# A two-layer trunk on one core: duos of the state-space layer spaced evenly, and the turn of its outputs written in the order of the tokens

## The chip, the cores and the metric

The kernel runs on one core of a Trainium2 chip. The metric is the device time of one execution in microseconds (us). Lower is better.

## The reference, cut to what matters

Two decoder layers work on 256 tokens of width 2048 in float32, each a token mixer, a SwiGLU feed-forward part and a gated per-layer embedding. The mixer of the second layer is the part that the change touches:

```python
def _s5_mixer(h, w_in, a_re, a_im, log_dt, b_re, b_im, c_re, c_im, d, w_out):
    u = (h @ w_in).astype(f32)                        # 256 x 2048
    ...
    bu = b_bar * u, per group of 16 channels, 64 complex states
    _, s = lax.associative_scan(_lin_combine, (a, bu), axis=1)
    y = Re(C s) + d * u                               # 256 x 2048
    g = jax.nn.gelu(y)
    val, gate = jnp.split(g @ w_out, 2, axis=-1)      # w_out is 2048 x 4096
    return val * jax.nn.sigmoid(gate)
```

## The kernel before, in words

All large products are done as a list of 783 weight tiles of 256 x 512 float32 (512 KB), `ORDER`, that every engine walks through. A float32 product is made of three: SyncE loads tile t into one of four slots (`RAW`), ScalarE rounds it to the high part (`WHI`, L779), VectorE subtracts that to get the low part (`WLO`, L1057), and TensorE multiplies the high part by both parts of the activations (8 matmuls, L1566) and the low part by the high part of the activations (4 matmuls, L1572). `section()` is this step on ScalarE and VectorE, and `until(t)` does it for all tiles to t + 2. A load of tile t waits for the low part of tile t - 4. ScalarE's rounding of tile t waits until TensorE is done with tile t - 4.

The stage `win` (h @ w_in) is tiles W0 to W0 + 31, eight for each of four columns of 512, and `out1` (g @ w_out) begins at W0 + 32. Below, "tile 40" is the tile W0 + 40. The work of the state-space layer is fitted between these tiles. Its 128 groups are taken in eight duos (d = 0 to 7) of 16 groups. TensorE does `into_states(d)` (64 small matmuls, L1758, the increments of the states) after tile `INTO_AT[d]`, and `out_of_states(d)` (96 small matmuls, L1775 and L1783, the outputs) after tile `OUT_AT[d]`. The order of the loops over g and the lists of places are written by hand. For each duo the chain is:

1. `into_states(d)` on TensorE;
2. `scan(d)` on VectorE, ten instructions, which begins with the transpose of the increments out of PSUM (`CV`, L1459) when VectorE has come to g = INTO + 1, that is after the low part of tile INTO + 3;
3. `out_of_states(d)` on TensorE, four tiles after the increments; for d = 6 and 7 it writes banks that are free only when VectorE has transposed the increments of duo 7;
4. `take_y(d)` on ScalarE at OUT + 1 (GELU, `YP`, L974);
5. `turn_y(d)` on VectorE at OUT + 2 (32 x 32 transposes, `YG`, L1485), after the low part of tile OUT + 4;
6. `y_high(d)` on ScalarE at OUT + 2 (L981), the high part of the operand, ahead of the rounding of tile OUT + 5;
7. `y_low(d)` on VectorE at OUT + 3 (L1490), after the low part of tile OUT + 5.

`out1` needs y as its operand: a tile (0, j), the j-th tile of column 0, waits for `y_low(j)`:

```python
if n == 0 and stage == "out1":
    pe.wait_ge(y_ready, j + 1)
```

`EARLY` orders the first three columns of `out1` so that tiles with a small j come first. Column 2 uses bank 6, and its first tile waits for `take_y(5)`.

The columns of u go to the states through DRAM: `turn_u(n)` on VectorE at 8n + 9 (L1451), `store_u(n)` (`ud`, L958) and `spread_u(n)` (`UP`, L966, four issues that wait for the store to land) on ScalarE's queue at 8n + 11 and 8n + 13. GpSimd's queue loads the tables TQ, TD, TK and TE of each duo at `TQ_AT`, `TD_AT`, `TK_AT` and `TE_AT`: 3.25 MB for a duo, beside 2 MB of weights in four tiles.

The layout of `YG` is (b, i, k): two blocks, the 8 tokens of a chunk, the 32 chunks. A token is 8k + i. So `y_high` and `y_low` read elements 128 bytes apart and write without gaps.

Of the kernel before, what the change touches and what calls it, by code (L numbers as in the profile page):

```python
# [6 lines left out]
F32 = mybir.dt.float32  # L7
F32R = mybir.dt.float32r
I32 = mybir.dt.int32
ACT = mybir.ActivationFunctionType  # L10
ALU = mybir.AluOpType
AX = mybir.AxisListType

P = 128
TOK = 256
# [16 lines left out]
T = 8  # L32
NC = TOK // T
# [11 lines left out]
PROJ_AT = 4  # L45

EARLY = [(n, j) for j in range(4) for n in (0, 1)] + [(2, j) for j in range(4)]
EARLY += [(n, j) for j in range(4, 8) for n in (0, 1, 2)]

def plan():
    order = []
    for name, cols, depth in STAGES:
        if name == "out1":
            order += [(name, n, j) for n, j in EARLY]
            order += [(name, n, j) for n in range(3, cols) for j in range(depth)]
# [11 lines left out]
def start(stage, n=0):  # L69
    return INDEX[stage, n, 0]  # L70
# [98 lines left out]

W0 = start("win")  # L170
U_AT = [W0 + 8 * n + 9 for n in range(NT)]
INTO_AT = [W0 + g for g in (16, 19, 24, 27, 32, 34, 40, 42)]
OUT_AT = [W0 + g for g in (20, 23, 28, 31, 36, 38, 44, 46)]

OUT_BANK = [6] * (DUOS - 2) + [4, 4]
Y_AT = [t + 2 for t in OUT_AT]
DSET = [0, 1, 2, 0, 1, 0, 1, 0]

G0 = start("gate0")
TQ_AT = [(G0 + 1, G0 + 3), (G0 + 13, G0 + 15)]  # L180
TD_AT = [(G0 + 5, G0 + 7), (G0 + 18, G0 + 20), (W0, W0 + 2)]
TK_AT = [(G0 + 9, G0 + 11), (G0 + 22, G0 + 24), (W0 + 4, W0 + 6)]
TE_AT = [G0 + 12, G0 + 26]
TQ_AT += [(W0 + g, W0 + g + 1) for g in (17, 20, 25, 28, 33, 35)]
TD_AT += [(W0 + g, W0 + g + 1) for g in (22, 26, 30, 37, 39)]
TK_AT += [(W0 + g, W0 + g + 1) for g in (24, 30, 32, 39, 41)]
TE_AT += [W0 + g for g in (20, 23, 28, 31, 36, 38)]

def set_before(d):  # L190
# [14 lines left out]
def trunk(nc, x, p, norm_mix, norm_ffn, norm_ple, norm_final, gm_w_in, gm_ln_g, gm_ln_b, gm_w_s, gm_b_s,  # L205
# [3 lines left out]
    with ctx:  # L209
        def sem(name):  # L210
            return ctx.enter_context(nc.semaphore(name))

        KBYTE = 1024
# [5 lines left out]
        def place(name, shape, dt=F32, at=None):  # L219
            size = 4  # L220
            for s in shape[1:]:
                size *= s
            if at is None:
                at = top[0]
                top[0] += (size + 31) // 32 * 32
                assert top[0] <= base + ARENA, name
            return nc.alloc_sbuf_tensor_at(name, shape, dt, offset=at)
# [3 lines left out]
        OP = place("OP", [P, 40, 2 * TOK], F32R)  # L231
# [3 lines left out]
        s_at = top[0]  # L235
# [28 lines left out]
        def f_view(name, shape, off, dt=F32):  # L264
            size = 4
            for s in shape[1:]:
                size *= s
            assert off * KBYTE + size <= 48 * KBYTE + 512, name
            return place(name, shape, dt, at=f_at + int(off * KBYTE))
# [65 lines left out]
        UP = [op_view(f"UP{i}", [P, 2, QB, QP, NC], 24 + 4 * i) for i in range(2)]  # L335

        YP = place("YP", [P, 2, T, 2, CH], at=s_at)
        YG = place("YG", [P, 2, T, NC], at=s_at + 2 * KBYTE)
        VAL = f_view("VAL", [P, 2, NW], 0)

# [89 lines left out]
        yg_ready = sem("yg_ready")  # L431
        y_hi = sem("y_hi")
        y_ready = sem("y_ready")
# [333 lines left out]
        def _(act):  # L767
            A_ = nc.scalar
# [200 lines left out]
            def take_y(d):  # L969
                act.wait_ge(out_of, d + 1)  # L970
                if d:
                    act.wait_ge(yg_ready, d)
                for g in range(2):
                    last = A_.activation(YP[:, :, :, g, :].rearrange("p b i c -> p b c i"),  # L974
                                         PS[:, OUT_BANK[d] + g, 0:2 * P].rearrange("p (b c i) -> p b c i", b=2, i=T),
                                         ACT.Gelu_apprx_tanh)
                last.then_inc(yp_ready, 1)

            def y_high(d):
                act.wait_ge(yg_ready, d + 1)  # L980
                A_.activation(OP[:, 2 * d:2 * d + 2, 0:TOK].rearrange("p b (k i) -> p b k i", i=T),  # L981
                              YG[:, :, :, :].rearrange("p b i k -> p b k i"), ACT.Copy).then_inc(y_hi, 1)

            for g in range(5, 62):
                until(W0 + g)
# [9 lines left out]
                for d in range(DUOS):  # L995
                    if W0 + g == Y_AT[d]:
                        y_high(d)
                    if W0 + g == OUT_AT[d] + 1:
                        take_y(d)
# [46 lines left out]
        def _(dve):  # L1046
            step = Chain(dve, dve_chain)
            V_ = nc.vector
# [274 lines left out]
            for n in range(NT):  # L1323
# [10 lines left out]
                for th in range(2):  # L1334
                    for m in range(QB):
                        h = QB * n + m
                        c = slice(P * m, P * m + P)
# [143 lines left out]
            def turn_y(d):  # L1481
                dve.wait_ge(yp_ready, d + 1)
                if d:
                    dve.wait_ge(y_ready, d)
                V_.transpose(YG[:, :, :, :].rearrange("p b i k -> p (b i k)"),  # L1485
                             YP[:, :, :, :, :].rearrange("p b i g c -> p (b i g c)")).then_inc(yg_ready, 1)

            def y_low(d):
                dve.wait_ge(y_hi, d + 1)
                V_.tensor_tensor(OP[:, 2 * d:2 * d + 2, TOK:2 * TOK].rearrange("p b (k i) -> p b k i", i=T),  # L1490
                                 YG[:, :, :, :].rearrange("p b i k -> p b k i"),
                                 OP[:, 2 * d:2 * d + 2, 0:TOK].bitcast(F32).rearrange("p b (k i) -> p b k i", i=T),
                                 ALU.subtract).then_inc(y_ready, 1)

            dve.wait_ge(core_ready, 1)
            until(W0 + 8)
# [2 lines left out]
            for g in range(7, 62):  # L1499
                until(W0 + g)  # L1500
                for n in range(NT):
                    if W0 + g == U_AT[n]:
                        turn_u(n)
                for d in range(DUOS):
                    if W0 + g == INTO_AT[d] + 1:
                        scan(d)
                    if W0 + g == Y_AT[d] + 1:
                        y_low(d)
                    if W0 + g == OUT_AT[d] + 2:
                        turn_y(d)  # L1510
                if W0 + g == end("out1", 1):
                    gated("out1", 1, VAL[:, :, :])
# [41 lines left out]
        def _(pe):  # L1554
# [191 lines left out]
            def into_states(d):  # L1746
                n, i = d // 2, d % 2
                pe.wait_ge(tq_in[i], 32 * (n + 1))
                pe.wait_ge(up_in, 64 * (n + 1))
                if d >= 2:  # L1750
                    pe.wait_ge(inc_free, d - 1)
                for bl in range(2):
                    for q in range(QP):
                        at = ST * (QP * bl + q)
                        for g in range(2):
                            for half in range(2):
                                state = ST * g + 32 * half
                                last = T_.matmul(PS[state:state + 32, 4 + i, at:at + ST], UP[n % 2][:, g, 2 * i + bl, q, :],  # L1758
                                                 TQ[i][:, bl, q, :, state:state + 32], start=True, stop=True)
                last.then_inc(in_done, 1)  # L1760

            def out_of_states(d):
                n, i, tab = d // 2, d % 2, DSET[d]
                pe.wait_ge(td_in[tab], 64 * (DSET[:d].count(tab) + 1))
                pe.wait_ge(sd_ready, d + 1)
                if d:
                    pe.wait_ge(yp_ready, d)
                if OUT_BANK[d] == 4:
                    pe.wait_ge(inc_free, DUOS)
                bank = OUT_BANK[d]  # L1770
                for bl in range(2):
                    f = slice(P * bl, P * bl + P)
                    for g in range(2):
                        for q in range(QP):
                            T_.matmul(PS[NC * q:NC * q + NC, bank + g, f], UP[n % 2][:, g, 2 * i + bl, q, :],  # L1775
                                      TKK[tab][:, bl, 2 * q + g, :], start=(bl == 0), stop=False, skip_group_check=True)
                for bl in range(2):
                    f = slice(P * bl, P * bl + P)
                    for ri in range(2):
                        for q in range(QP):  # L1780
                            for g in range(2):
                                half = slice(ST * g, ST * g + ST)
                                last = T_.matmul(PS[NC * q:NC * q + NC, bank + g, f], SD[i][half, ri, QP * bl + q, :],  # L1783
                                                 TD[tab][half, bl, q, ri, :], start=False, stop=(ri == 1), skip_group_check=True)
                last.then_inc(out_of, 1)

            for t in range(W0, INDEX["out1", 2, 7] + 1):
# [12 lines left out]
                for d in range(DUOS):  # L1800
                    if t == INTO_AT[d]:
                        into_states(d)
                    if t == OUT_AT[d]:
                        out_of_states(d)
# [55 lines left out]
```

## Time and profile before

| what | value |
|---|---|
| time, median of 3 runs | 2246.61 us (2244.24 to 2249.15) |
| the profiled execution: its own time | 2250.04 us |
| its span | 2248.0 us |
| TensorE busy with matmuls | 2229.2 us (99%) |
| VectorE busy | 1442.2 us (64%) |
| ScalarE busy | 1021.1 us (45%) |
| DMA over the span | 235 GB/s |
| granted TensorE clock, mean | 0.998 |

Tile 16 starts in this trace at 1166.45 us and tile 48 at 1289.36 us. A time is read against the start of the span. The difference of own time and span, 2.04 us, lies around the profiled program.

### The profile page before, as it was taken

To read this page: it belongs to the slowest core of one execution; us is meant where nothing else is said; L and a number is where in the kernel's file an instruction comes from. 1 tells how busy PE (TensorE), PEld (TensorE's weight loads), DVE (VectorE), ACT (ScalarE), POOL (GpSimd) and SP (SyncE) were. 2 spreads that over 40 slices of the span, in tenths; PEclk is the share of its full clock that TensorE was granted. 3 is DMA by queue.
4 is the path that set the end of the run, shared out by engine and by line. 5 is a ranking of instruction groups with operands and counts; after the bars stand their busy time and mean duration, and the time that the engine had idled before them with its cause. 6 is when DMAs were issued, how large, how long until landed. Compare 5 with 4: busy or idle time off the path is not lost.

```text
span 2248.0 us, 28342 instructions
## 1 busy us (share of the span) xinstructions
PE 2229.2 (99%) x11250; PEld 1834.4 (82%) x11250; DVE 1442.2 (64%) x1590; ACT 1021.1 (45%) x1233; POOL 494.0 (22%) x469
## 2 busy tenths in 40 slices
PE   9999999999999999999999999999999999999998
PEld 7888878888888888888887788888888888888886
DVE  7878776667666666666668766555555445555665
ACT  5544454444434444445444455444444344444444
POOL 1245236455665544301003100000000000000001
PEclk9999999999999999999999999999999999999999
DMA  8667799888887888887779877677766667777764
GB/s 288 188 206 232 242 274 269 245 245 254 248 247 219 259 259 245 249 256 265 236 250 338 302 220 222 198 222 217 217 213 214 191 195 221 219 215 232 227 213 143
DMA packets 348517, 527.90 MB, mean 235 GB/s; under 512 B 105968, under 2 KB 125312, under 8 KB 347744
## 3 DMA queue, kind: packets, MB, share of 16 engines
q1 hardware_dynamic: 337296, 488.50, 71.4%
q0 software_dynamic: 8320, 30.75, 3.8%
q10 hardware_dynamic: 2768, 6.83, 0.9%
q8 instruction: 89, 1.46, 0.3%
q14 instruction: 44, 0.36, 0.1%
HBM read 474.10 MB, written 51.90 MB: 234 GB/s over the span
## 4 chain that ended last, share of the span: by engine, by line
PE 90%; DVE 4%; DMA 3%; issue 1%; ACT 1%; SPq 1%; DVEq 0%; ACTq 0%
PE PS L1566 58%; PE PS L1572 29%; DVE WLO L1057 1%; DMA HT<-zd 1%; DMA RAW<-in_s_w_out 1%; DMA RAW<-in_ffn_w 1%; ACT WHI L779 0%; PE PS L1597 0%; DMA RAW<-in_s_w_in 0%; PE PS L1669 0%; PE PS L1837 0%; PE PS L1838 0%; PE PS L1836 0%; DVE CB L1469 0%; PE PS L1660 0%
## 5 line engine op out<-in xcount | busy, mean ns | idle before, releaser
L1566 PE MATMUL PS<-WHI,OP 128*128 128x512 f32 x6208 | 1541.3, 390 | 1.4 <-ACT WHI L779 1.1
L1057 DVE TENSOR_TENSOR WLO<-RAW,WHI 128x1024 fp32r<-128x1024 f32 x783 | 1022.2, 1317 | 660.8 <-ACT WHI L779 657.9
L1566 PEld LDWEIGHTS PS<-WHI,OP 128*128 128x128 f32 x6208 | 1161.7, 188 | 248.1 <-issue 6.6
L779 ACT ACTIVATE WHI<-RAW 128x1024 fp32r<-128x1024 f32 x783 | 825.4, 1061 | 936.0 <-PE PS L1572 759.6
L1572 PE MATMUL PS<-WLO,OP 128*128 128x512 f32 x3104 | 830.7, 389 | 3.8 <-DVE WLO L1057 3.6
L1572 PEld LDWEIGHTS PS<-WLO,OP 128*128 128x128 f32 x3104 | 582.2, 188 | 127.1 <-DVE WLO L1057 6.1
L763 POOL TENSOR_TENSOR ON<-X,GF 128x1024 f32<-128x1024 f32 x3 | 9.9, 3291 | 947.8 <-DVE X L1406 947.8
L666 POOL TENSOR_TENSOR TA<-BRAW,FAC 128x64 f32<-128x64 f32 x16 | 8.2, 512 | 259.8 <-DMA BRAW<-in_s_b_im 259.8
L1069 DVE TENSOR_TENSOR OP<-HT,OP 128x512 fp32r<-128x512 f32 x50 | 34.9, 739 | 46.7 <-ACT OP L794 46.7
L794 ACT ACTIVATE OP<-HT 128x512 fp32r<-128x512 f32 x50 | 28.8, 624 | 65.3 <-DMA HT<-zd 65.3
L827 ACT ACTIVATE S<-PS,RC 128x512 f32<-128x512 f32 x66 | 41.8, 685 | 36.5 <-PE PS L1572 36.5
L1083 DVE SCALAR_TENSOR_TENSOR OP<-HT,VEC,OP 128x128 fp32r<-128x128 f32 x96 | 26.3, 347 | 32.1 <-ACT OP L803 32.1
L803 ACT ACTIVATE OP<-HT,VEC 128x256 fp32r<-128x256 f32 x48 | 20.5, 498 | 35.9 <-DMA HT<-zd 35.9
L1393 DVE SCALAR_TENSOR_TENSOR Z<-PS,RC,S 128x512 f32<-128x512 f32 x44 | 30.9, 744 | 6.0 <-PE PS L1572 5.2
L1124 DVE BATCH_NORM_STATS2 STAT<-X 128x6 f32<-128x512 f32 x54 | 34.1, 673 | 0.0
L1108 DVE STREAM_TRANSPOSE ZT<-Z 128x512 f32<-128x512 f32 x50 | 32.6, 691 | 0.9
L913 ACT ACTIVATE EXPF<-PS 128x128 f32<-128x128 f32 (+7 forms) x128 | 17.8, 264 | 33.2 <-PE PS L1669 33.2
L698 POOL TENSOR_TENSOR TA<-CT,LAMA 128x512 f32<-128x512 f32 x16 | 18.1, 1134 | 60.8 <-DMA CT<-cd 60.8
L701 POOL TENSOR_TENSOR TA<-CT,LAMA 128x512 f32<-128x512 f32 x16 | 31.0, 1936 | 1.3
L700 POOL TENSOR_TENSOR DT<-TA,TB 128x512 f32<-128x512 f32 x16 | 31.0, 1936 | 1.3
L685 POOL TENSOR_TENSOR QT<-TA,TB 128x512 f32<-128x512 f32 x16 | 30.5, 1908 | 1.3
L702 POOL TENSOR_TENSOR TB<-CT,LAMA 128x512 f32<-128x512 f32 x16 | 29.9, 1869 | 0.0
(213 smaller groups left out, 961.6 us busy)
## 6 DMA issues: line engine op xcount, KB each, us to landing
RAW<-in_ffn_w SPq DMA_DIRECT2D x528, 512.0 KB, 4.7
RAW<-in_gm_w_in SPq DMA_DIRECT2D x64, 512.0 KB, 4.7
RAW<-in_ple_w_gate SPq DMA_DIRECT2D x64, 512.0 KB, 4.8
RAW<-in_s_w_out SPq DMA_DIRECT2D x64, 512.0 KB, 5.2
zd<-ZT SPq DMA_DIRECT2D x37, 512.0 KB, 4.1
HT<-zd SPq DMA_DIRECT2D x148, 128.0 KB, 5.5
RAW<-in_gm_w_out SPq DMA_DIRECT2D x32, 512.0 KB, 5.3
RAW<-in_s_w_in SPq DMA_DIRECT2D x32, 512.0 KB, 6.1
```

The lines of the kernel that those rows point to most:

```text
L685: G_.tensor_tensor(QT[:, :, 1, :, :], TA[:, :, :, :], TB[:, :, :, :], ALU.add).then_inc(q_ready, 1)
L700: step(G_.tensor_tensor(DT[:, :, 0, :, :], TA[:, :, :, :], TB[:, :, :, :], ALU.add))
L701: G_.tensor_tensor(TA[:, :, :, :], c(1), up(0), ALU.mult)
L779: A_.activation(hi_of(t), RAW[:, t % RING, :], ACT.Copy).then_inc(hi_ready, 1)
L827: last = A_.activation(dst(th), acc(stage, n)[:, th, :], func, scale=RC[:, RMS[stage], th:th + 1])
L1057: V_.tensor_tensor(lo_of(t), RAW[:, t % RING, :], hi_of(t).bitcast(F32), ALU.subtract).then_inc(lo_ready, 1)
L1069: V_.tensor_tensor(here[:, :, TOK + P * h:TOK + P * h + P].rearrange("p m (i a) -> p m i a", a=32), HT[:, :, :, h, :].rearrange("p i m a - ...
L1108: last = V_.transpose(ZT[:, :, :, h, :], src[:, h, :].rearrange("p (m c a) -> p c m a", c=4, a=32))
L1124: last = V_.bn_stats(STAT[:, th, 6 * n:6 * n + 6], src[:, th, NW * n:NW * n + NW])
L1393: last = V_.scalar_tensor_tensor(Z[:, th, :], acc(stage, n)[:, th, :], RC[:, i_rms, th:th + 1], S[:, th, :], ALU.mult, ALU.mult)
L1566: T_.matmul(dst[:, th, :], x_part, WHI[:, slot, f], start=first and kk == 0 and part == 0, stop=False)
L1572: last = T_.matmul(dst[:, th, :], hi, WLO[:, slot, f], start=False, stop=last_one and kk == TK - 1)
```

## The change

- `INTO_AT` goes from (16, 19, 24, 27, 32, 34, 40, 42) to (16, 20, 24, 28, 32, 36, 40, 43), and `OUT_AT` from (20, 23, 28, 31, 36, 38, 44, 46) to (20, 24, 28, 32, 36, 40, 44, 47). So the outputs of duo d and the increments of duo d + 1 stand behind the same tile for d = 0 to 5, outputs first.
- The lists of table loads follow.
- `EARLY` puts tiles (0, 4) and (1, 4) of `out1` at 40 and 41, ahead of column 2, whose first four tiles move from 40 to 43 to 42 to 45. Before, (0, 4) was tile 44.
- `YG` becomes (b, k, i). `turn_y` writes elements 32 bytes apart, and `y_high` and `y_low` read without gaps.

```diff
-EARLY = [(n, j) for j in range(4) for n in (0, 1)] + [(2, j) for j in range(4)]
-EARLY += [(n, j) for j in range(4, 8) for n in (0, 1, 2)]
+EARLY = [(n, j) for j in range(5) for n in (0, 1)] + [(2, j) for j in range(5)]
+EARLY += [(n, j) for j in range(5, 8) for n in (0, 1, 2)]
...
-INTO_AT = [W0 + g for g in (16, 19, 24, 27, 32, 34, 40, 42)]
-OUT_AT = [W0 + g for g in (20, 23, 28, 31, 36, 38, 44, 46)]
+INTO_AT = [W0 + g for g in (16, 20, 24, 28, 32, 36, 40, 43)]
+OUT_AT = [W0 + g for g in (20, 24, 28, 32, 36, 40, 44, 47)]
...
-TQ_AT += [(W0 + g, W0 + g + 1) for g in (17, 20, 25, 28, 33, 35)]
-TD_AT += [(W0 + g, W0 + g + 1) for g in (22, 26, 30, 37, 39)]
-TK_AT += [(W0 + g, W0 + g + 1) for g in (24, 30, 32, 39, 41)]
-TE_AT += [W0 + g for g in (20, 23, 28, 31, 36, 38)]
+TQ_AT += [(W0 + g, W0 + g + 1) for g in (17, 21, 25, 29, 33, 37)]
+TD_AT += [(W0 + g, W0 + g + 1) for g in (22, 26, 34, 38, 41)]
+TK_AT += [(W0 + g, W0 + g + 1) for g in (24, 30, 36, 40, 43)]
+TE_AT += [W0 + g for g in (20, 24, 28, 32, 36, 40)]
...
-        YG = place("YG", [P, 2, T, NC], at=s_at + 2 * KBYTE)
+        YG = place("YG", [P, 2, NC, T], at=s_at + 2 * KBYTE)
...
-                V_.transpose(YG[:, :, :, :].rearrange("p b i k -> p (b i k)"),
-                             YP[:, :, :, :, :].rearrange("p b i g c -> p (b i g c)")).then_inc(yg_ready, 1)
+                V_.transpose(YG[:, :, :, :].rearrange("p b k i -> p b i k"),
+                             YP[:, :, :, :, :].rearrange("p b i g c -> p b i (g c)")).then_inc(yg_ready, 1)
```

In `y_high` and `y_low` the reading pattern `"p b i k -> p b k i"` of `YG` becomes `"p b k i -> p b (k i)"`, with nothing else changed.

## Rows read from the trace of the kernel before

**Rows 1.** The page: engines, busy us, share of the span, instructions.

```profile
PE 2229.2 (99%) x11250; PEld 1834.4 (82%) x11250; DVE 1442.2 (64%) x1590; ACT 1021.1 (45%) x1233; POOL 494.0 (22%) x469
```

**Rows 2.** Waits of TensorE, whole kernel: us in total, times, longest.

```profile
PE PS L1572 <- DVE WLO L1057: 3.6, 3, 1.8
```

**Rows 3.** Timeline of TensorE, undisturbed part of the stage: start, us, what.

```profile
1163.73 1.98 PE L1566 MATMUL PS<-WHI,OP 128*128 128x512 f32 x8
...
1166.45 1.98 PE L1566 MATMUL PS<-WHI,OP 128*128 128x512 f32 x8
...
1173.14 1.98 PE L1566 MATMUL PS<-WHI,OP 128*128 128x512 f32 x8
...
1187.60 1.98 PE L1566 MATMUL PS<-WHI,OP 128*128 128x512 f32 x8
```

**Rows 4.** Timeline of TensorE, later in the same stage.

```profile
1249.78 1.21 PE L1572 MATMUL PS<-WLO,OP 128*128 128x512 f32 x4 [1.69 <-DVE WLO L1057]
...
1273.47 1.19 PE L1572 MATMUL PS<-WLO,OP 128*128 128x512 f32 x4 [1.76 <-DVE WLO L1057]
1275.32 1.94 PE L1775 MATMUL PS<-TK,UP 128*32 128x128 f32 x32 [0.66 <-DVE CV L1459]
1277.19 1.59 PE L1783 MATMUL PS<-TD,SD 64*32 64x128 f32 x64
1278.71 2.14 PE L1566 MATMUL PS<-WHI,OP 128*128 128x512 f32 x8
...
1289.36 1.98 PE L1566 MATMUL PS<-WHI,OP 128*128 128x512 f32 x8
```

**Rows 5.** Windows: length, busy us by engine, granted clock, DMA share, GB/s.

```profile
1228.00:1259.00 31.00, 29.15 (x416) 22.61 (x404) 26.12 (x35) 12.35 (x16) 12.21 (x17) 1.00 1.01 381
1275.00:1276.00 1.00, 0.68 (x16) 0.71 (x20) 0.96 (x3) 0.00 (x0) 0.00 (x0) 0.50 0.85 317
```

**Rows 6.** Timeline of VectorE in the stage.

```profile
1171.29 0.67 DVE L1459 STREAM_TRANSPOSE CV<-PS 128x512 f32<-128x512 f32 x1
...
1177.54 3.69 DVE L1057 TENSOR_TENSOR WLO<-RAW,WHI 128x1024 fp32r<-128x1024 f32 x3
...
1222.60 0.70 DVE L1485 STREAM_TRANSPOSE YG<-YP 128x512 f32<-128x512 f32 x1
1225.42 1.23 DVE L1057 TENSOR_TENSOR WLO<-RAW,WHI 128x1024 fp32r<-128x1024 f32 x1 [2.12 <-ACT WHI L779]
1226.57 1.22 DVE L1490 TENSOR_TENSOR OP<-YG,OP 128x512 fp32r<-128x512 f32 x1
1227.72 1.35 DVE L1057 TENSOR_TENSOR WLO<-RAW,WHI 128x1024 fp32r<-128x1024 f32 x1
...
1230.55 1.24 DVE L1451 STREAM_TRANSPOSE UT<-Z 128x1024 f32<-128x1024 f32 x1
```

**Rows 7.** Instructions on YG: ns least/median/most, first and last start.

```profile
L1485 DVE STREAM_TRANSPOSE YG<-YP x8: 670/704/706, 1189.7 to 1290.3; 128x512 f32<-128x512 f32 x8
L981 ACT ACTIVATE OP<-YG x8: 1100/1148/1172, 1190.4 to 1291.0; 128x512 fp32r<-128x512 f32 x8
L1490 DVE TENSOR_TENSOR OP<-YG,OP x8: 1090/1111/1221, 1194.2 to 1294.3; 128x512 fp32r<-128x512 f32 x8
```

**Rows 8.** The same for two operand splits that read runs of 32 elements.

```profile
L794 ACT ACTIVATE OP<-HT x50: 614/618/634, 147.3 to 2048.5; 128x512 fp32r<-128x512 f32 x50
L1069 DVE TENSOR_TENSOR OP<-HT,OP x50: 682/690/1795, 148.0 to 2049.2; 128x512 fp32r<-128x512 f32 x50
```

**Rows 9.** Timeline of ScalarE and its DMA issues in the stage.

```profile
1203.83 0.33 ACTq L958 DMA_DIRECT2D ud<-UT  x1
...
1211.48 2.75 ACTq L966 DMA_DIRECT2D UP<-ud  x4
1214.34 1.14 ACT L974 ACTIVATE YP<-PS 128x256 f32<-128x256 f32 x2 [1.88 <-PE PS L1783]
```

**Rows 10.** DMA issues in 1160 to 1300: count, size, median us to landing.

```profile
RAW<-in_s_w_in SPq DMA_DIRECT2D x13, 512.0 KB, 8.1
```

More of the change, by code:

```diff
@@ L980, in y_high @@
                 act.wait_ge(yg_ready, d + 1)
-                A_.activation(OP[:, 2 * d:2 * d + 2, 0:TOK].rearrange("p b (k i) -> p b k i", i=T),
-                              YG[:, :, :, :].rearrange("p b i k -> p b k i"), ACT.Copy).then_inc(y_hi, 1)
+                A_.activation(OP[:, 2 * d:2 * d + 2, 0:TOK], YG[:, :, :, :].rearrange("p b k i -> p b (k i)"), ACT.Copy).then_inc(y_hi, 1)
             for g in range(5, 62):
@@ L1484, in turn_y @@
                     dve.wait_ge(y_ready, d)
-                V_.transpose(YG[:, :, :, :].rearrange("p b i k -> p (b i k)"),
-                             YP[:, :, :, :, :].rearrange("p b i g c -> p (b i g c)")).then_inc(yg_ready, 1)
+                V_.transpose(YG[:, :, :, :].rearrange("p b k i -> p b i k"),
+                             YP[:, :, :, :, :].rearrange("p b i g c -> p b i (g c)")).then_inc(yg_ready, 1)
             def y_low(d):
                 dve.wait_ge(y_hi, d + 1)
[L1490 to L1493, printed above, removed]
+                V_.tensor_tensor(OP[:, 2 * d:2 * d + 2, TOK:2 * TOK], YG[:, :, :, :].rearrange("p b k i -> p b (k i)"),
+                                 OP[:, 2 * d:2 * d + 2, 0:TOK].bitcast(F32), ALU.subtract).then_inc(y_ready, 1)
             dve.wait_ge(core_ready, 1)
```

## The prediction, made before the changed kernel had run

> **What bounds the kernel now.** I read the page first: TensorE is busy for 99% of the span and no other engine comes near [rows 1]. So only time in which TensorE waits or works slowly can be won. The waits of TensorE came next. Nearly all that lie between the start and the end of the program belong to one stage, where VectorE brings the low part of a weight tile too late, three times, 3.6 us in all [rows 2]. That is the stage that the change touches, so I went to TensorE's timeline there.
>
> The cadence of undisturbed tiles is 1166.45 - 1163.73 = 2.72 us [rows 3]. From 1166.45 (tile 16) to 1173.14 (tile 18) are two tiles and one pass of increments: 6.69 - 5.44 = 1.25 us for the pass. From 1166.45 to 1187.60 (tile 22) are six tiles, two such passes and one of outputs: 21.15 - 16.32 - 2.50 = 2.33 us for the outputs [rows 3]. Tile 48 starts at 1289.36 [rows 4], so tiles 16 to 47 and all passes took 122.91 us, where 32 x 2.72 + 8 x (1.25 + 2.33) = 115.7 would do. **The stage loses 7.2 us**, 0.32% of the time. The reader is to see where in [rows 4]: 1.69 us at tile 38 and 1.76 us at tile 44 for the low part, 0.66 us for the transpose of duo 7's increments (`CV`), and then the outputs pass of duo 6, which takes 1278.71 - 1275.32 = 3.39 us instead of 2.33 with the clock granted at 0.50, the 1.2 GHz level, after TensorE had stood still [rows 5]. The last is some 1.1 to 1.3 us. The rest are parts of a microsecond around tiles 28, 31 and 40.
>
> Why VectorE is late is in its timeline. A scan takes from 1171.29 to 1177.54, 6.25 us [rows 6], and in the old lists some scans follow after two or three tiles.
>
> **The change, part by part.**
>
> *Spacing.* Every duo but the last now has a round of four tiles. TensorE's round is 4 x 2.72 + 1.25 + 2.33 = 14.46 us less what the shared place saves. Two passes behind one tile save one change-over between large and small matmuls. No row has two passes together. Below, nothing is saved; above, 0.25 us, a fifth of the 1.25 us of a pass. I take 0.2 us, by the row of the pass. Six pairs: **-1.2 us**, bounds 0 and -1.5. The round is 14.26 us.
>
> VectorE's round is one scan, four sections, one turn and one `y_low`, and a wait in its middle: after `turn_y` the next section needs a high part that ScalarE rounds only after `y_high`. Now the turn starts at 1222.60 and that section at 1225.42, 2.82 us; a section's step is 1.15 (1225.42 to 1226.57) and `y_low`'s too (1226.57 to 1227.72) [rows 6].
>
> *The layout.* `y_high` takes 1.15 us and `y_low` 1.11 reading with gaps [rows 7]. Splits of the same size that read runs of 32 elements take 0.62 and 0.69 [rows 8]. So ScalarE gains 0.53 and VectorE 0.42 to 0.5 per duo. The turn, 0.70 us now [rows 7], gets the gaps on its write side. No row shows a transpose that writes single elements. Below, it stays at 0.70; above, it pays what `y_low` paid for its reads and more, 1.15. I take 1.05, nearer the upper end, since the gap of 32 bytes is like the old one in that no two neighbours are adjacent. Of 2.82 us the handover becomes 2.82 + 0.35 - 0.53 = 2.64, and `y_low`'s step 0.65. VectorE's round: 6.25 + 4 x 1.15 + 2.64 + 0.65 = **14.14 us** against TensorE's 14.26. It just fits. But every second round has `turn_u` too, 1.2 us [rows 6]. It comes before the scans of duos 2 and 4. VectorE's lag behind the end of the increments is then 1.1 us at scan 2, 1.0 at scan 3, 2.0 at scan 4 and 1.9 at scan 5.
>
> The Trainium skill (Advanced Engine Details and Errata, SBUF Cachelines) says that SBUF is fast only where accesses fall at least twice into the same 16 bytes. The dear reads of [rows 7] agree. By it the turn's writes at 32 bytes pay the whole price, about 1.12 us, and the sum would end 0.2 us higher; with no price on writes it would end about 1 us lower. No row here shows which.
>
> *What the lag costs on the way.* The low part of tile 36 is wanted 3 x 2.72 + 0.14 + 1.81 = 10.1 us after the increments of duo 4 and is there after 0.1 + 2.0 + 6.25 + 1.15 = 9.5. So the waits at tiles 28, 38 and 44 go: **-7.2 us** (with the clock's share). Waits of parts of a microsecond may come at tile 32, whose high part stands on ScalarE behind `spread_u(2)`, and at 36: 0 to 2 us, I take **+0.3**.
>
> *`EARLY`.* Tile 40 is now (0, 4) and waits for `y_low(4)`; before, tile 44 did. Counted from the end of duo 5's increments (behind tile 36, after duo 4's outputs), TensorE comes to tile 40 after 3 x 2.72 + 0.14 = 8.3 us. VectorE: scan 5 starts at 0.1 + 1.9 and ends at 8.25; low part of tile 40, 9.4; turn to the next section, 12.0; that section, 13.2; `y_low`, 13.9. **TensorE waits 5.6 us.** On top comes ScalarE's queue: `spread_u(3)` waits for the store `ud`, and `take_y(4)` and the high part of tile 40 stand behind it. Store to spread took 1211.48 - 1203.83 = 7.65 us, the four issues 2.75, `take_y` 1.14 [rows 9]. The store of u's last column goes out 11.2 us into duo 4's round (0.1 + 2.0 + 6.25 + 1.15 + turn 1.05 + `y_high` 0.62), so the high part of tile 40 is ready at 11.2 + 7.65 + 2.75 + 1.14 + 1.0 = 23.7. VectorE wants it at 14.26 + 8.25 = 22.5. That adds 0 to 1.3, I take 0.9: **+6.5 us** at tile 40. Its lower bound is 3.4 (turn at 0.70 us, no lag left at scan 5, no delay by ScalarE), its upper 9 (turn at 1.15 and late weights).
>
> *The clock.* After that stop the first microseconds run at 1.2 GHz, as after the stop at 1273 [rows 4, 5]: at least 1.1, at most double. **+1.5 us.**
>
> *The end.* The outputs of duo 6 wait for the transpose of duo 7's increments. From the end of duo 6's increments TensorE is there after 8.3 + 1.25 + 2.8 = 12.4 us. VectorE, which has caught up by now, has 0.1 + 6.25 + 3 x 1.15 + 2.64 + 0.65 + 0.70 = 13.8. **+1.4 us**, bounds 0.8 and 2.2. Before, it was 0.66 [rows 4], part of the 7.2.
>
> *DMA.* In 1228 to 1259 the transfers ran at 381 GB/s with a share of 1.01 [rows 5], and a weight tile took 8.1 us to land in the stage [rows 10], more than half a round. The new lists spread the same bytes a little later. A slot's round of 14.3 us has room for 8.1 + 1.1 + 1.2, so I take 0. GpSimd's queue: the loads for duos 3, 5 and 7 now wait for increments behind outputs, 2.3 us longer, and come six tiles (over 16 us) before use: 0.
>
> **Sum**: -7.2 - 1.2 + 0.3 + 6.5 + 1.5 + 1.4 = **+1.3 us**. The profiled execution would go from 2250.04 to 2251.3 us (span 2248.0 to 2249.3). It stood 3.4 us above the median of the runs, 2246.61; from that the forecast is 2247.9, put at 2248.0 us.
>
> **The rivals.**
>
> 1. *The operand comes nearly in time* (faster). If VectorE has no lag and ScalarE no delay, the wait is 3.4 us, the sum -7.2 - 1.2 + 3.4 + 1.1 + 0.8 = -3.1, 2243.5 us. If the wait fell to 0, the clock stayed too: -7.2 - 1.2 + 1.4 = -7.0, 2239.6 us. It crosses the bound of 0.2% (4.5 us) where tile 40 waits less than 2.5 us. For it: waits now are short. Against it: the chain of 12 to 14 us stands against 8.3.
> 2. *Late weights* (slower). The share of DMA is at its limit in part of the stage [rows 5]. If tiles land after 11 to 12 us instead of 8, high parts come late at 32 and 40: wait at tile 40 of 9 us, 2 more at 32 and 36, clock 2, end 1.6: -8.4 + 9 + 2 + 2 + 1.6 = +6.2, 2252.8 us. It decides from a landing of some 11 us on.
> 3. *The waits before stay.* The spacing does not free VectorE, because its round with `turn_u` is 15.3 us against 14.26, and 2 to 3 us of low-part waits remain beside tile 40's: +1.3 + 2.5, 2250.4 us.
>
> **How the numbers follow.** Chances: forecast 0.50, rival 1 0.17, rival 2 0.23, rival 3 0.10. A measurement of this kernel can tell 0.2%, 4.5 us, from no change. The forecast's own spread (wait of 4.5 to 8 us) is -1 to +3.5, same with 0.44 and slower with 0.06. Rival 1: 0.13 faster, 0.04 same. Rival 2: 0.05 same, 0.18 slower. Rival 3: 0.06 same, 0.04 slower. Together faster 0.13, same 0.59, slower 0.28. The range of 8 in 10 reaches into rivals 1 and 2: 2242 to 2254 us.
>
> **What would show it.** TensorE's waits after: none on `WLO` at tiles 38 and 44, one long wait of L1566 for `OP` by L1490 (`y_low`) at tile 40, a window at clock 0.50 behind it, and about 1.4 us of L1775 for `CV` L1459. `YG` by its turn at 1.05 us, `OP` from `YG` at 0.62 on ScalarE and 0.69 on VectorE. Wrong would be: no wait at tile 40, because VectorE is ahead; a turn far above 1.15 us, since each 0.1 us there adds 0.1 to the round and some 0.3 to tile 40; or waits of TensorE on `WHI` by DMA.

## The result, and the profile after

In 11 runs each the changed kernel took 2252.97 us (2249.45 to 2257.27) and the kernel before 2246.61 us (2244.24 to 2251.00). The ratio is **1.0024, interval 1.0016 to 1.0032**: slower by about 5.4 us by the ratio, 6.4 by the medians. The forecast was 2248.0 us in a range of 2242 to 2254. The change made the kernel slower, which had a chance of 0.28; a change too small to measure had 0.59. The 0.2% at which the prediction drew the line between the two lies inside the interval. The profiled execution took 2252.43 us with a span of 2250.7 us.

The waits of TensorE in the stage (us in total, times, longest), changed kernel. They answer to [rows 2]:

```profile
PE PS L1563 <- DVE OP L1489: 3.7, 1, 3.7
PE PS L1755 <- issue: 2.0, 1, 2.0
PE PS L1772 <- DVE CV L1458: 1.6, 1, 1.6
```

No wait for `WLO` is left. The first row is the wait that the prediction put at tile 40, shorter than forecast; the third is the one that it put at the end. The second was in no sum: "issue" means that TensorE stood still and the profile shows nothing that it waited for. Its timeline says where (start, us, what, and the idle time before it):

```profile
1219.72 1.98 PE L1563 MATMUL PS<-WHI,OP 128*128 128x512 f32 x8
...
1222.53 1.08 PE L1772 MATMUL PS<-TK,UP 128*32 128x128 f32 x32
1223.54 1.16 PE L1780 MATMUL PS<-TD,SD 64*32 64x128 f32 x64
1224.62 0.97 PE L1755 MATMUL PS<-TQ,UP 128*32 128x64 f32 x52
1227.55 0.42 PE L1755 MATMUL PS<-TQ,UP 128*32 128x64 f32 x12 [1.95 <-issue]
1227.90 3.68 PE L1563 MATMUL PS<-WHI,OP 128*128 128x512 f32 x8
1231.42 1.09 PE L1569 MATMUL PS<-WLO,OP 128*128 128x512 f32 x4
1232.34 1.98 PE L1563 MATMUL PS<-WHI,OP 128*128 128x512 f32 x8
...
1255.94 3.78 PE L1563 MATMUL PS<-WHI,OP 128*128 128x512 f32 x8 [3.72 <-DVE OP L1489]
1259.52 1.91 PE L1569 MATMUL PS<-WLO,OP 128*128 128x512 f32 x4
1261.36 1.43 PE L1772 MATMUL PS<-TK,UP 128*32 128x128 f32 x32
1262.72 1.16 PE L1780 MATMUL PS<-TD,SD 64*32 64x128 f32 x64
1263.80 1.10 PE L1755 MATMUL PS<-TQ,UP 128*32 128x64 f32 x64
1264.83 2.11 PE L1563 MATMUL PS<-WHI,OP 128*128 128x512 f32 x8
...
1278.92 1.08 PE L1772 MATMUL PS<-TK,UP 128*32 128x128 f32 x32 [1.65 <-DVE CV L1458]
```

Behind tile 32 both passes follow each other, and in the middle of the increments, after 52 of 64 matmuls of one kind, TensorE stops for 1.95 us; all that the pass waits for stands in the program ahead of its first matmul. The tile behind the stop then takes 1232.34 - 1227.90 = 4.44 us, where the one behind an undisturbed pair takes 2.89. After the longer stop the tile, both passes and all took 1264.83 - 1255.94 = 8.89 us, where the undisturbed one with the pair behind tile 24 took 5.94. The windows (columns as in [rows 5]) show why both are slow: the clock is granted at 0.50, the 1.2 GHz level:

```profile
1229.00:1230.00 1.00, 1.00 (x4) 0.81 (x3) 0.97 (x3) 0.40 (x1) 0.11 (x1) 0.50 1.06 385
1257.00:1258.00 1.00, 1.00 (x4) 0.81 (x3) 0.02 (x1) 0.16 (x1) 0.00 (x0) 0.50 1.04 410
```

The instructions on `YG` (ns least/median/most), which answer to [rows 7]:

```profile
L1484 DVE STREAM_TRANSPOSE YG<-YP x8: 1125/1150/1155, 1190.4 to 1294.8; 128x512 f32<-128x512 f32 x8
L981 ACT ACTIVATE OP<-YG x8: 629/632/633, 1191.6 to 1296.0; 128x512 fp32r<-128x512 f32 x8
L1489 DVE TENSOR_TENSOR OP<-YG,OP x8: 683/684/1035, 1194.4 to 1298.8; 128x512 fp32r<-128x512 f32 x8
```

The gaps have moved as foretold, and the turn pays for them at the upper bound, 1.15 us.

**The account.** From the start of tile 16 to the start of tile 49 TensorE needs 118.4 us by the cadences of [rows 3]. Before it took 125.63, now 129.61: +4.0 us. The old losses are gone (-7.2), and six pairs save 0.18 to 0.2 each (-1.1). The wait at tile 40 adds 3.9 (6.60 us between tile starts instead of 2.72), the slow clock behind it 2.95 (8.89 - 5.94), the stop behind tile 32 adds 3.8 (8.18 - 5.94 for tile 32 with its passes, and 4.44 - 2.89 for the next), the end 1.7 (6.75 - 5.05, the latter 2.72 + 2.33). The sum is 4.1, against the +4.0 measured. The two stretches of slow clock are not the same in every execution: experiment 10, the same kernel once more, has the same stops and waits with less of it.

### The profile page after: what moved, and what is told of

Its sections match the earlier page's. It is cut to its first block, busy times and chain, and to the rows that moved or that the text cites. A ratio compares the mean times of both kernels' runs of the same rounds, so it can differ in the third digit from the quotient of the medians.

```text
span 2250.7 us, 28344 instructions
## 1 busy us (share of the span) xinstructions
PE 2228.6 (99%) x11250; PEld 1835.6 (82%) x11250; DVE 1443.2 (64%) x1590; ACT 1014.9 (45%) x1233; POOL 500.1 (22%) x469
## 4 chain that ended last, share of the span: by engine, by line
PE 92%; DVE 3%; DMA 2%; issue 1%; ACT 1%; SPq 0%; ACTq 0%
PE PS L1563 60%; PE PS L1569 30%; DVE WLO L1056 1%; DMA HT<-zd 1%; DMA RAW<-in_ple_w_gate 0%; PE PS L1666 0%; PE PS L1594 0%; PE PS L1780 0%; PE PS L1772 0%; DMA X<-in_x 0%; PE PS L1755 0%; PE PS L1657 0%; DMA RAW<-in_ffn_w 0%; DVE OP L1082 0%; DMA RAW<-in_ple_w_proj 0%
## 5 line engine op out<-in xcount | busy, mean ns | idle before, releaser
L703 POOL TENSOR_TENSOR DT<-TA,TB 128x512 f32<-128x512 f32 x16 | 32.0, 2002 | 1.3
L700 POOL TENSOR_TENSOR DT<-TA,TB 128x512 f32<-128x512 f32 x16 | 31.9, 1992 | 1.3
```

Source lines behind the costliest of these rows:

```text
L700: step(G_.tensor_tensor(DT[:, :, 0, :, :], TA[:, :, :, :], TB[:, :, :, :], ALU.add))
L703: G_.tensor_tensor(DT[:, :, 1, :, :], TA[:, :, :, :], TB[:, :, :, :], ALU.subtract).then_inc(d_ready, 1)
```

## The experiments

Times are medians with lowest and highest; ratios are to the kernel before, run beside them.

**1. The lists alone.** `YG` and the three instructions on it go back to the old form, the new lists stay.

```diff
-        YG = place("YG", [P, 2, NC, T], at=s_at + 2 * KBYTE)
+        YG = place("YG", [P, 2, T, NC], at=s_at + 2 * KBYTE)
```

> The new lists of places with the old layout of YG. Theory A (the changed layout gives VectorE about 0.5 us per round of four tiles, since y_low falls by 0.43 us, y_high by 0.5 and the turn rises by 0.45): VectorE's round is about 14.75 us instead of 14.2, it lags more when scan 5 begins, and tile 40 waits 4 to 6 us instead of 3.7; the time is 1 to 3 us above the changed kernel, 2254 to 2256 us. Rival B (the dearer turn eats what the split gains, and the layout is worth nothing): the same as the changed kernel within 1 us. In both, the 1.95 us break inside the increments behind tile 32 stays, because TensorE's list of instructions is the same.

2253.74 us (2252.42 to 2256.55), ratio 1.0033 (1.0020 to 1.0046). The waits of TensorE in the stage:

```profile
PE PS L1566 <- DVE OP L1490: 6.5, 1, 6.5
PE PS L1775 <- DVE CV L1459: 2.2, 1, 2.2
PE PS L1758 <- issue: 1.3, 1, 1.3
```

All the loss is in the lists, and so is the stop, again after 52 matmuls behind tile 32.

**2. The layout alone.** The new `YG`, the old lists.

```diff
-OUT_AT = [W0 + g for g in (20, 24, 28, 32, 36, 40, 44, 47)]
+OUT_AT = [W0 + g for g in (20, 23, 28, 31, 36, 38, 44, 46)]
```

> The new layout of YG with the old lists. Theory A: VectorE gains up to 0.5 us before scan 5 and before scan 6, so the two waits of 1.7 us for low parts at tiles 38 and 44 shrink to about 1.2 each; 1 to 2 us below the kernel before, 2244.5 to 2246 us. Rival B: no change, 2246.6. Rival C (the layout itself is what made the change slower): above 2249.

2245.58 us (2242.69 to 2248.15), ratio 0.9993 (0.9984 to 1.0002): no measurable change. The waits for `WLO` at tiles 38 and 44 are shorter, 1.17 and 0.61 us instead of 1.69 and 1.76 [rows 4]. The kernel before has no wait at tile 38 in its second trace (experiment 9), so only the one at tile 44 says something. This is the whole stage:

```profile
PE PS L1569 <- DVE WLO L1056: 1.8, 2, 1.2
PE PS L1772 <- DVE CV L1458: 0.7, 1, 0.7
PE PS L1563 <- ACT YP L974: 0.5, 1, 0.5
```

```diff
-            for _ in range(12):
+            for _ in range(76):
                 T_.transpose(PS[:, 3, 0:P], IDENT[:, :], IDENT[:, :])
```

> The changed kernel with 64 more warm-up transposes at TensorE's start (76 instead of 12), which shift every later TensorE instruction by 128 places in its list and cost some 8 to 15 us at the start. Theory D (the break behind tile 32 is a late transfer of TensorE's own instructions: the page counts 89 transfers on the instruction queue for 1.46 MB, 16 KB each, and 22,500 matmuls and weight loads over 88 of them are 256 instructions or 128 matmuls each; counted so, one block of the changed kernel begins at matmul 22 of the outputs pass and ends at matmul 54 of the increments pass behind tile 32, and the break came after 52): the break leaves tile 32, whose pair then holds only one boundary, and if the transfers are busy there it comes up behind tile 36, after 36 to 38 matmuls of the increments, where a block lies wholly inside the pair. Rival E (the break is a chance event or belongs to the tables or to the tile): it stays after 52 matmuls behind tile 32, or appears at no such place.

One run, 2257.77 us (it includes the added transposes). TensorE's timeline:

```profile
1221.77 0.86 PE L1563 MATMUL PS<-WHI,OP 128*128 128x512 f32 x3 [1.57 <-issue]
...
1247.98 0.69 PE L1755 MATMUL PS<-TQ,UP 128*32 128x64 f32 x33
1249.02 0.65 PE L1755 MATMUL PS<-TQ,UP 128*32 128x64 f32 x31 [0.35 <-issue]
```

The stop left tile 32. It stands in tile 29 after 5 matmuls, where the blocks now have a boundary at 6, and a short one of 0.35 us behind tile 36 after 33, where one was due at 36 to 38. Data, buffers and the order of work are the same in both kernels.

**4. `y_low` early.** VectorE does the turn and `y_low` right after the scan, so that tile 40's operand is there.

```diff
-                    if W0 + g == Y_AT[d] + 1:
-                        y_low(d)
-                    if W0 + g == OUT_AT[d] + 2:
+                for d in range(DUOS):
+                    if W0 + g == OUT_AT[d] + 1:
                         turn_y(d)
+                        y_low(d)
```

> The changed kernel, but VectorE does turn_y and y_low of a duo directly after the scan that stands at the same place, ahead of the next low part of a weight tile (one and two tiles earlier). Theory A (tile 40 waits for the chain scan, low part, turn, high part of a tile, low part, y_low): 2.3 to 3 us leave that chain, the wait at tile 40 falls from 3.7 to about 1 us, the slow microseconds behind it shrink or go, and the wait before the outputs of duo 6 falls by some 0.7; 4 to 6 us below the changed kernel, 2247 to 2249 us. Rival F (VectorE's total work sets it, wherever y stands): the wait moves to a low part of a tile and the time stays at 2251 to 2253. The break behind tile 32 stays in both.

2248.78 us (2244.44 to 2250.66), ratio 1.0005 (0.9996 to 1.0014). The waits:

```profile
PE PS L1755 <- issue: 3.7, 2, 2.1
PE PS L1772 <- DVE CV L1458: 1.1, 1, 1.1
PE PS L1563 <- DVE OP L1489: 0.6, 1, 0.6
PE PS L1569 <- issue: 0.3, 1, 0.3
```

The wait at tile 40 fell from 3.7 to 0.6 us, and with it the slow clock behind it; some 4 us came back. What the profile calls issue grew to 4.0: stops after 52 matmuls behind tile 32, after 5 behind tile 28, and 0.3 us in tile 26.

```profile
1202.82 0.62 PE L1569 MATMUL PS<-WLO,OP 128*128 128x512 f32 x2 [0.30 <-issue]
...
1213.01 1.08 PE L1755 MATMUL PS<-TQ,UP 128*32 128x64 f32 x59 [1.68 <-issue]
...
1231.85 0.42 PE L1755 MATMUL PS<-TQ,UP 128*32 128x64 f32 x12 [2.05 <-issue]
```

All three are at block boundaries: counted in TensorE's list they stand 127 and 255 matmuls apart, one block and two. But the block before the one behind tile 28 had begun in the tiles and not run through in 2.5 us, so a whole block inside a pair is not the only case.

**5. Passes in places of their own.** Outputs three tiles behind the increments, increments one tile behind the outputs: rounds of four stay, the pairs go. ScalarE and VectorE deal with y two tiles behind the outputs, before the next scan; `spread_u` comes one tile later, and the loads of TD and TK move to fit. What each of these is worth is not separated.

```diff
-OUT_AT = [W0 + g for g in (20, 24, 28, 32, 36, 40, 44, 47)]
+OUT_AT = [W0 + g for g in (19, 23, 27, 31, 35, 39, 44, 47)]
...
-                    if W0 + g == Y_AT[d] + 1:
-                        y_low(d)
                     if W0 + g == OUT_AT[d] + 2:
                         turn_y(d)
+                        y_low(d)
+                for d in range(DUOS):
+                    if W0 + g == INTO_AT[d] + 1:
+                        scan(d)
```

> The changed kernel with the outputs three tiles after the increments for duos 0 to 5 (behind 19, 23, 27, 31, 35, 39), so that no two passes stand behind one tile, take_y and y_high two tiles after the outputs, and turn_y and y_low at that place ahead of the scan of the next duo, in the time in which VectorE waits for its increments; spread_u one tile later, the loads of TD and TK moved to fit. Theory A: the chain to y_low(4) no longer holds a scan and ends before tile 39 does, so tile 40 does not wait; the scan of duo 7 is reached before the outputs of duo 6 need it; VectorE's round is some 13.5 us against TensorE's 14.46. TensorE waits under 1 us in the stage and the clock stays up. About 7 us below the kernel before, 2239 to 2241.5 us. Theory D (breaks come where TensorE runs through a block of 128 matmuls faster than its next block lands): none of more than 0.5 us, since at most one pass stands between tiles. Rival G (transfers bound the stage: earlier use of the tables makes TensorE or ScalarE wait for DMA): a wait of 1 to 4 us for TD or TK or for high parts, 2244 to 2247.

2241.73 us (2239.52 to 2247.74), ratio 0.9986 (0.9977 to 0.9995): **faster than both kernels**. It is 3 to 4 us below the kernel before, about half of the 7 expected. The only wait left in the stage, and then a window over it:

```profile
PE PS L1771 <- issue: 0.6, 1, 0.6
```

```profile
1165.00:1285.00 120.00, 119.38 (x1681) 95.00 (x1681) 106.82 (x142) 53.74 (x65) 30.44 (x44) 1.00 0.93 336
```

TensorE stands still for 0.62 us in 120 and the clock stays at 1.00. From the start of tile 16 to that of tile 49 it takes 119.08 us. There is no stop within a pass. The word issue hides something else here, as the last instruction of the scan and the outputs that read it show:

```profile
1249.49 0.41 DVE L1476 TENSOR_TENSOR SD<-CV,CA 128x248 f32<-128x248 f32 x1
```

```profile
1250.00 1.08 PE L1771 MATMUL PS<-TK,UP 128*32 128x128 f32 x32 [0.62 <-issue]
```

The scan ends at 1249.90, TensorE goes on at 1250.00: this is a wait for the scan. The distance of three tiles is just enough, this wait apart.

**6. The same with the old `YG`.**

```diff
-        YG = place("YG", [P, 2, NC, T], at=s_at + 2 * KBYTE)
+        YG = place("YG", [P, 2, T, NC], at=s_at + 2 * KBYTE)
```

> The same with the old layout of YG. Theory A: VectorE's round keeps half a microsecond or more of slack, so the layout is worth nothing here, the same as e5_three_apart within 1 us. Rival (the layout matters wherever y stands): 2 to 3 us more than it.

2245.56 us (2241.55 to 2249.44), ratio 1.0002 (0.9993 to 1.0011), 3.8 us above experiment 5. The scan's last instruction and the outputs of duo 4:

```profile
1235.11 0.40 DVE L1477 TENSOR_TENSOR SD<-CV,CA 128x248 f32<-128x248 f32 x1
```

```profile
1235.62 1.08 PE L1774 MATMUL PS<-TK,UP 128*32 128x128 f32 x32 [2.33 <-issue]
```

By the medians the layout counts here, with turn and `y_low` in VectorE's chain just before the scan, though the intervals of the two ratios still overlap a little. TensorE wanted this scan at 1235.62 - 2.33 = 1233.29, and it ended at 1235.51, 16.77 us after the outputs of duo 3 had begun (1218.74). In experiment 5 the same stretch is 1234.72 - 1220.41 = 14.31 us, within TensorE's round of 14.45. Of the 2.46 us between the two, 0.5 are the layout's own: from the start of the turn to the scan it is 2.94 us here (1226.07 to 1229.01) and 2.43 in experiment 5 (1226.04 to 1228.47). The rest is not placed. Nor does this one profile show the 3.8: its execution took 2242.17 us, that of experiment 5 2241.62. The expectation that the layout is worth nothing there failed by the medians.

**7. Is the stop a matter of full transfer queues?** The loads of `TD` and `TKK` for duos 3 to 7 are cut to a sixteenth and an eighth. This leaves out part of the tables: the rest keeps older values, and only the time is of use.

```diff
+                few = slice(0, QP * 2 * P if d < 3 else 64)
...
+                few = slice(0, GB if d < 3 else 1)
```

> The changed kernel with the same instructions, but the loads of TD and TK for duos 3 to 7 bring only a sixteenth and an eighth of each table (that part of the computation is left out: old values stand in the rest). Some 4.8 MB less moves in the stage. Theory D (the break behind tile 32 is TensorE's own instructions landing late among full transfer queues): the break after 52 matmuls goes, although TensorE's list is the same. Theory A then also says that VectorE no longer catches up during the break, so its lag at scan 5 is 1.5 to 2.5 us and tile 40 waits longer than 3.7 us, 5 to 6.5. Rival E (the break belongs to the pair itself, not to the transfers): it stays. Time: 0 to 3 us below the changed kernel.

2250.18 us (2249.32 to 2251.84), ratio 1.0022 (1.0011 to 1.0033). The window ahead of and in the stop, first the changed kernel, then this one:

```profile
1223.00:1227.00 4.00, 2.60 (x140) 2.04 (x130) 3.92 (x4) 3.98 (x6) 0.00 (x0) 1.00 1.02 375
```

```profile
1223.00:1227.00 4.00, 2.50 (x133) 2.05 (x130) 3.92 (x5) 4.00 (x7) 0.00 (x0) 1.00 0.67 217
```

The share of the transfers fell from 1.02 to 0.67, but the stop stayed at its matmul with 1.50 us for 1.95, and the expectation that it goes failed. Experiment 1, with full tables, stopped for 1.31 us, so even the difference of 0.45 may be chance. The load of the tables does not make the stop. The transfers of 1225 to 1226 in the changed kernel, by queue (packets, MB, share), hold the one instruction packet that came between 1212 and 1231:

```profile
q8 instruction: 1, 0.02, 6.8%
```

In windows of 0.1 us it is counted between 1225.1 and 1225.2 (the view does not say whether this is its start or its end). The 52 matmuls are through at 1225.6, and TensorE goes on at 1227.55, 2.4 us behind the packet. All seven traces with pairs have this distance at every stop (times in us):

| execution | stop | last packet | TensorE goes on | apart |
|---|---|---|---|---|
| changed kernel | 1.95 | 1225.1 | 1227.55 | 2.4 |
| experiment 1 | 1.31 | 1224.4 | 1226.87 | 2.5 |
| experiment 3 | 1.57 | 1219.4 | 1221.77 | 2.4 |
| experiment 3 | 0.35 | 1246.5 | 1249.02 | 2.5 |
| experiment 4 | 0.30 | 1200.5 | 1202.82 | 2.3 |
| experiment 4 | 1.68 | 1210.6 | 1213.01 | 2.4 |
| experiment 4 | 2.05 | 1229.5 | 1231.85 | 2.3 |
| experiment 7 | 1.50 | 1224.0 | 1226.54 | 2.5 |
| experiment 8 | 1.76 | 1192.1 | 1194.57 | 2.5 |
| experiment 10 | 1.94 | 1224.7 | 1227.17 | 2.5 |

So a stop ends 2.3 to 2.5 us behind a packet, whatever its length. The pair behind tile 20 of the changed kernel also holds a whole block and runs undisturbed: there the packet came at 1178.2, some 4 us before the block's end was reached at about 1182.4. The waits of experiments 5 and 6 are not of this kind: the last packets stood at 1246.6 and 1228.4, 3.4 and 7.2 us before TensorE went on.

The Trainium skill (Advanced Engine Details and Errata, ISA Cache) says that a cache line is 16 KB, which is 256 instructions. The size agrees with the 256 worked out above. It also says that there are only two lines, but gives TensorE 128 KB beside 32 KB, which by its line size would be eight; no run shows the number of lines.

**8. Shifted by 96**, 108 transposes instead of 12.

```diff
-            for _ in range(12):
+            for _ in range(108):
```

> The changed kernel with 96 more warm-up transposes at the start, which cost some 10 us there and move every later TensorE instruction by 192 places, so that no block of 128 matmuls lies wholly inside the pair of passes behind tile 32. Theory D (the breaks come where a block of TensorE's own instructions is run through faster than the next one lands, about 4 to 5 us after TensorE's queue reached it): no break behind tile 32 nor behind 36. Without the break VectorE does not catch up at scan 4, its lag at scan 5 is 2 us or more, and tile 40 waits 5 to 6.5 us instead of 3.7. Rival E: a break of 1 to 2 us stays in the increments behind tile 32.

One run, 2260.09 us, with the added transposes. TensorE's timeline:

```profile
1194.57 1.20 PE L1569 MATMUL PS<-WLO,OP 128*128 128x512 f32 x4 [1.76 <-issue]
...
1264.69 3.73 PE L1563 MATMUL PS<-WHI,OP 128*128 128x512 f32 x8 [6.38 <-DVE OP L1489]
```

With no stop behind tile 32 or 36, tile 40 waits 6.38 us; 6.5 were forecast as that term of the sum. 1.31 us of this chain are VectorE's wait for the high part of tile 40, which stood behind `spread_u(3)` and `take_y(4)` on ScalarE, as the forecast had it with 0.9. A new stop stands in tile 21 after 8 of its 12 matmuls, where a boundary was due after 6, behind the pair of tile 20, most of whose matmuls lay in one block. It comes before VectorE has any lag to make up (VectorE waited 2.3 us for the increments there), and so takes nothing off tile 40.

**9 and 10. Both kernels once more**, unchanged, side by side.

> The kernel before, unchanged, profiled a second time, to see how far one profile stands for all: three waits for low parts of 3 to 4 us in all and 1.7 us late at tile 44, no break inside a pass. From the start of tile 16 to that of tile 49 within 1 us of the 125.6 us of the first profile. If the first was a poor sample, it is 2 us or more shorter.

> The changed kernel, unchanged, profiled a second time: the break after 52 matmuls behind tile 32 again (it stands at a fixed place in the list), the wait at tile 40 at 3.5 to 5 us, the wait before the outputs of duo 6 at 1.6. From the start of tile 16 to that of tile 49 within 1 us of the 129.6 us of the first profile.

2249.32 us before and 2248.94 after, one run each: single runs say nothing of 0.2%. The stage took 123.45 and 126.91 us, 3.5 apart (4.0 in the first pair). Each was expected within 1 us of its first profile, and is 2.2 and 2.7 shorter. Before, the wait at tile 38 is absent this time, the one at tile 44 is again 1.8 us. After, the waits are the same:

```profile
PE PS L1563 <- DVE OP L1489: 4.0, 1, 4.0
PE PS L1755 <- issue: 1.9, 1, 1.9
PE PS L1772 <- DVE CV L1458: 1.6, 1, 1.6
```

What differs is the clock. Behind the stop of 1.94 us it stays at 1.00 and the next tile takes 2.86 us, where it took 4.44. Behind the wait at tile 40 the tile with its passes takes 7.50 us, where it took 8.89. These two make 3.0 us.

```profile
1227.52 2.11 PE L1563 MATMUL PS<-WHI,OP 128*128 128x512 f32 x8
...
1254.26 3.52 PE L1563 MATMUL PS<-WHI,OP 128*128 128x512 f32 x8 [4.00 <-DVE OP L1489]
...
1261.76 2.11 PE L1563 MATMUL PS<-WHI,OP 128*128 128x512 f32 x8
```

## Why the prediction was right and wrong

The time fell inside the range, above the forecast, and in part because errors cancelled: against the sum of +1.3 the stage measured +4.0, with 2.6 less than forecast at tile 40, 1.45 more for the clock behind it and 3.8 from a stop that was in no sum.

- **Old waits, -7.2.** Right: none on `WLO` is left. But 7.2 was one execution; in experiment 9 the same kernel loses about 5.0 us in the stage (123.45 - 118.4), so the forecast counted a gain of which some 2 us come and go.
- **Shared place, -1.2.** Measured -1.1 in time. What the pair costs besides was not seen.
- **VectorE's round, 14.14 us.** Measured 1212.77 - 1198.57 = 14.20 between two scans. The turn took 1.15 us (forecast 1.05), and the handover, which holds it, 2.80 (2.64); most of this 0.16 is made up by shorter steps. The estimate by the rule of the Trainium skill (Advanced Engine Details and Errata, SBUF Cachelines), 1.12 us, was nearer than my choice.
- **Tiles 32 and 36, +0.3.** No wait there in either profile of the changed kernel. The term was not needed.
- **Tile 40, +6.5.** Place, instruction and chain right, the size not: 3.7 and 4.0 us. By the forecast's own chain the operand comes 13.9 us after duo 5's increments, of which 1.9 are lag. Measured 12.1 (1243.79 to 1255.89). The lag was away, because TensorE's stop behind tile 32 had given VectorE time. Where the stop is away, the wait is 6.4 (experiment 8); with the old `YG` it is 6.5 in spite of the stop. The 0.9 us for ScalarE's queue were not needed in the changed kernel, where `take_y(4)` ran at 1245.53, long before; in experiment 8 they came, with 1.31.
- **The clock, +1.5.** 2.95 us in the first profile, 1.56 in experiment 10 of the same kernel (7.50 - 5.94). In the four other executions with a wait of 4 to 6.5 us there it is 1.7 to 2.9 (experiments 1, 3, 7 and 8). Read as 1.1 to 3.0, the bounds held; that the choice of 1.5 is near one of the two profiles is luck.
- **The end, +1.4.** 1.65 us, right.
- **Rival 2, late weights**, gave nearly the measured time (2252.8 us) by a mechanism that did not occur: weight tiles landed faster than before, after a median of 6.5 us from `in_s_w_in` (8.1 in [rows 10]), and TensorE never waited for one in the changed kernel's profile. **Rival 1** is what experiment 4 made: wait at tile 40 nearly gone, yet only no change, as the stops ate its gain. **Rival 3** did not come.
- **What stays open.** The stage explains 3.5 to 4.0 us of the 5.4 (by the ratio). Single profiles of one kernel scatter by 2 to 3 us in this stage, in the changed kernel by the slow clock, so the rest can't be placed.

## What to carry to other kernels

Count what a stage issues as well as what it computes: behind passes of small matmuls joined into runs of 160, TensorE stopped in all seven executions, and with the passes kept apart by a tile in none of five. When outputs move later, ask which tile needs what comes out of them and count the whole chain up to it. A wait that goes away gives its time to the engines behind it, and so two new waits of a sum are not independent: each shortens the one that follows.

## What the runs showed of the hardware

- A transpose on VectorE of 128x512 pays 1.15 us instead of 0.70 when it writes single elements 32 bytes apart; reads 128 bytes apart cost `y_high` 1.15 instead of 0.63 and `y_low` 1.11 instead of 0.68.
- With pairs of passes (160 small matmuls in a row) TensorE stops with no wait that the profile shows, ten times in seven executions, for 0.3 to 2.05 us. In the five that are not shifted a stop of 1.31 to 2.05 us stands after 52 of 64 matmuls behind tile 32; in the shifted ones (experiments 3 and 8) it stands elsewhere. The three stops of experiment 4 are 127 and 255 matmuls apart.
- Each of these stops ends 2.3 to 2.5 us behind a packet of 16 KB on the queue that the page calls "instruction".
- After a stop of 3.7 us the granted clock is 0.50 up to about 1262, some 6 us, at a cost of 2.95 us; after one of 4.0 in experiment 10 the cost is 1.56.
- Of the ten short stops two were followed by the clock at 0.50: the 1.95 us of the changed kernel (some 3.5 us, at a cost of 1.55) and the 1.68 of experiment 4. Behind the 1.94 of experiment 10 and the 2.05 of experiment 4 it stayed at 1.00.
- "issue" in the waits can be a wait for another engine: in experiments 5 and 6 outputs began 0.10 and 0.11 us after the scan's end.
